# Base addresses of the operand tiles in a hybrid retention and attention layer

## The reference, cut to what matters

```python
h = rms_norm(x, g_pre_mix)
proj = h @ w_in                      # 1024 x 3072
rq, rk, rv, rg, aq, ak, av = split(proj)
ret = retention_branch(rq, rk, rv, rg, positions)          # 512 wide, chunks of 128
att = dilated_attention_branch(aq, ak, av, positions)      # 512 wide, dilations 1, 4, 16
mix = concatenate([ret, att]) @ w_out
x = x + rms_norm(mix, g_post_mix)
h = rms_norm(x, g_pre_ffn)
f = (silu(h @ w_gate) * (h @ w_up)) @ w_down               # D_FF = 2816
x = x + rms_norm(f, g_post_ffn)
```

## Time and profile before

| | |
|---|---|
| median of three runs | 2846.91 us |
| profiled execution, its own time | 2851.44 us |
| its span | 2849.7 us |
| TensorE busy | 2653.0 us, 93% |
| VectorE / ScalarE / GpSimd busy | 43% / 25% / 22% |
| mean granted TensorE clock | 0.963 |

### The profile page before, as it was taken

How to read it: one execution, slowest core, us unless ns; L and a number is a source line. 1 busy time by engine, 2 the same in 40 slices (tenths; PEclk the granted TensorE clock), 3 DMA queues, 4 the chain that set the end, 5 groups by cost and what they waited for, 6 DMA issues and landing times. The chain is left out here.

```text
span 2849.7 us, 36155 instructions
## 1 busy us (share of the span) xinstructions
PE 2653.0 (93%) x13096; PEld 2229.4 (78%) x13096; DVE 1231.6 (43%) x2271; ACT 722.1 (25%) x1402; POOL 627.2 (22%) x403
## 2 busy tenths in 40 slices
PE   6999999959989879997799999999999999999995
PEld 5888877749989757776588888888888888888884
DVE  5213455215655588885233333333354333333334
ACT  4112111116766522222211111111121111111111
POOL 1793544112344166663000000000010000000000
PEclk8999999979999989999899999999999999999998
DMA  4321233255335335553611111111352111111103
GB/s 164 97 73 61 79 110 110 96 140 128 103 102 172 115 112 178 175 179 123 243 45 45 59 59 44 44 44 45 117 185 82 45 44 54 64 44 44 44 15 103
DMA packets 220448, 269.66 MB, mean 95 GB/s; under 512 B 12224, under 2 KB 164672, under 8 KB 220096
## 3 DMA queue, kind: packets, MB, share of 16 engines
q1 hardware_dynamic: 220352, 268.42, 30.0%
HBM read 188.29 MB, written 80.08 MB: 94 GB/s over the span
## 5 line engine op out<-in xcount | busy, mean ns | idle before, releaser
L1418 PE MATMUL ff_psum_gu<-ff_h_hi,ff_w_hi 128*128 128x512 f32 x1408 | 550.5, 391 | 21.7 <-DMA ff_h_lo<-h_lo 21.7
L1418 PE MATMUL ff_psum_gu<-ff_h_lo,ff_w_hi 128*128 128x512 f32 x1408 | 550.1, 391 | 0.0
L1418 PE MATMUL ff_psum_gu<-ff_h_hi,ff_w_lo 128*128 128x512 f32 x1408 | 550.0, 391 | 0.0
L1523 POOL TENSOR_TENSOR ff_ssq<-ff_ssq,ff_minus_half 128x1 f32<-128x1 f32 x16 | 14.4, 905 | 1467.0 <-DVE ff_ssq L1564 1467.0
L1544 DVE TENSOR_TENSOR ff_gated<-ff_gated,ff_psum_gu 128x512 f32<-128x512 f32 x88 | 60.5, 687 | 628.8 <-PE ff_psum_gu L1418 628.8
L1418 PEld LDWEIGHTS ff_psum_gu<-ff_h_hi,ff_w_hi 128*128 128x128 f32 x1408 | 265.6, 189 | 77.6 <-issue 18.6
L327 PE MATMUL pr_psum_acc<-pr_hT_hi,pr_w_hi 128*128 128x512 f32 x768 | 304.6, 397 | 12.4 <-DVE pr_w_lo L234 12.4
L1418 PEld LDWEIGHTS ff_psum_gu<-ff_h_hi,ff_w_lo 128*128 128x128 f32 x1408 | 265.5, 189 | 55.3
L1418 PEld LDWEIGHTS ff_psum_gu<-ff_h_lo,ff_w_hi 128*128 128x128 f32 x1408 | 265.5, 189 | 55.0
L327 PE MATMUL pr_psum_acc<-pr_hT_lo,pr_w_hi 128*128 128x512 f32 x768 | 302.3, 394 | 0.0
L327 PE MATMUL pr_psum_acc<-pr_hT_hi,pr_w_lo 128*128 128x512 f32 x768 | 302.0, 393 | 0.0
(11 more groups left out here) (159 smaller groups left out, 3969.6 us busy)
## 6 DMA issues: line engine op xcount, KB each, us to landing
ff_raw<-in_w_gate SPq DMA_DIRECT2D x22, 1024.0 KB, 5.4
ff_raw<-in_w_up SPq DMA_DIRECT2D x22, 1024.0 KB, 7.8
ff_down_raw<-in_w_down SPq DMA_DIRECT2D x22, 1024.0 KB, 4.9
projT<-pr_rows SPq DMA_DIRECT2D x64, 256.0 KB, 2.4
att_out<-at_orow SPq DMA_DIRECT2D x192, 66.0 KB, 1.7
mx_att_in<-att_out SPq DMA_DIRECT2D x16, 792.0 KB, 4.8
pr_w_raw<-in_w_in SPq DMA_DIRECT2D x24, 512.0 KB, 4.3
nt_xin<-in_x SPq DMA_DIRECT2D x16, 512.0 KB, 5.0
```

The source lines that it names most:

```text
L1418: last = nc.tensor.matmul(gu_ps[:, tile, n], w[:, n, k, cols], h[:, k, t], start=i == 0, stop=i == 3 * KT - 1)
L1523: nc.gpsimd.tensor_tensor(ssq[:, c], ssq[:, c], minus_half[:], ALU.pow).then_inc(rooted, 1)
```

## The change

Four gap tiles are allocated (one in projection, three in the FFN), which nothing reads or writes, and two tiles of `mix` are declared further up. No instruction is added, removed or put elsewhere.

```diff
@@ project
         raw = m.sb("w_raw", [P, KT, P])
+        m.sb("gap", [P, 64])
         w_hi = m.sb("w_hi", [P, 2, KT, P], F32R)
         w_lo = m.sb("w_lo", [P, 2, KT, P], F32R)
@@ mix
         w_lo = m.sb("w_lo", [P, KT, DM], F32R)
+        mT_hi = m.sb("mT_hi", [P, 2, KT, P], F32R)
+        mT_lo = m.sb("mT_lo", [P, 2, KT, P], F32R)
         ident = m.sb("ident", [P, P])
...
         mixT = m.sb("mixT", [P, 4, P])
-        mT_hi = m.sb("mT_hi", [P, 2, KT, P], F32R)
-        mT_lo = m.sb("mT_lo", [P, 2, KT, P], F32R)
@@ ffn
         raw = m.sb("raw", [P, 2, KT, PW])
+        m.sb("gap0", [P, 96])
         w_hi = m.sb("w_hi", [P, 2, KT, PW], F32R)
         w_lo = m.sb("w_lo", [P, 2, KT, PW], F32R)
+        m.sb("gap1", [P, 32])
         down_raw = m.sb("down_raw", [P, TILES, DM])
         down_hi = m.sb("down_hi", [P, TILES, DM], F32R)
         down_lo = m.sb("down_lo", [P, TILES, DM], F32R)
         gated = m.sb("gated", [P, TILES, GROUP])
+        m.sb("gap2", [P, 112])
         a_hi = m.sb("a_hi", [P, UG, TILES, GROUP], F32R)
         a_lo = m.sb("a_lo", [P, UG, TILES, GROUP], F32R)
```

## The result

The changed kernel takes 2877.28 us (median of 4 runs, 2875.53 to 2883.28) against 2847.88 us before; the ratio is 1.0102, 95% interval 1.0079 to 1.0125. The profiled execution's span is 2881.5 us against 2849.7. The forecast was no change (2846.5); the time lies inside the range of 8 in 10, on the slower side.

What follows compares the result with a forecast made beforehand. TensorE was taken to bound projection and FFN, VectorE to pace mix. Terms of 0 for projection and FFN, -0.4 us for mix and 0 for moved operands took the median 2846.91 to 2846.5 us; range 2815 to 2893 us.

Steps and rivals of the forecast that it cites:

- The step to price by: Projection and FFN: price a matmul by its time from start to start, 226.7 ns, not by its duration of about 391.
- I take 0 for all three: Projection, gate and up, and down: the gaps' new differences change no step; 0 us, within bounds of -113 to +63.
- a coarse difference only shifts when the two reads are close: Projection and FFN: reason for the 0; differences of 64 bytes or more don't change how often weight load and moving read meet.
- a start off a multiple of 64: Mix's output product: its 234.1 ns step put down to a difference below 64 bytes or mT's start off 64.
- slower rival: Projection and FFN: unequal differences down to 64 bytes raise steps towards 234.1 ns; +63 us in full, 2910 us; chance 0.28.
- The one unequal row in the trace: Mix's output product before the change: operands 352 bytes apart by 512, step 234.1 ns against 226.7 elsewhere.
- if the unit is 256 bytes: Case of the slower rival: projection keeps its step, both FFN products pay; +46 us, 2893 us.
- faster rival: Projection and FFN: equal remainders collide, so the 13.3 ns extra falls to 2.3; -93 us, 2754 us; chance 0.20.
- one faster stage: Case of the faster rival: one stage alone gains, -25 us (projection, 2822), -46 (gate and up) or -23 (down).
- Mix: Mix's output product: step falls from 234.1 to 226.7 ns, mostly hidden in a wait; -0.4 us, bounds 0 and -5.2.
- Moved operands of other engines cost 0: VectorE and ScalarE split and copy the same tiles at other starts; 0 us.

Runs made afterwards that it cites:

- e4: Kernel before with all of projection's tiles 32 bytes further and all of the FFN's 96, both operands still at a difference of 0; ratio 0.9999.
- e3: Gaps resized against the kernel before, for differences by 256 bytes of 192 (projection), 96 (gate and up), 128 (down), 192 (mix); 2899.35 us, ratio 1.0185.
- e11: The changed kernel with gaps of 64 elements everywhere, so every stationary-to-moving difference is 256 bytes; ratio 1.0002 against the kernel before.
- the map: Table of steps by stationary-to-moving difference by 256 bytes, from runs with other gap sizes or sliced tiles against the kernel before; 226.7 to 234.2 ns.
- e10: Kernel before with each down matmul of 512 columns split into two of 256, addresses as before; 2875.27 us, ratio 1.0099.
- e8: Only the low weights (w_lo) of projection and of gate and up moved 128 bytes further, against the kernel before; ratio 1.0093.
- e14: Gate and up's 24 matmuls grouped in eights by operand pair, with its w_lo 128 bytes further, against the kernel before; ratio 1.0030.
- e15: Only gate and up's low moving tile (h_lo) moved 128 bytes further, in the old order, against the kernel before; ratio 1.0024.
- e7: Stationary tiles sliced from wider ones, for differences of 8 bytes (projection), 16 (FFN) and 4 (mix), against the kernel before; 2875.54 us, ratio 1.0099.
- e9: Both low tiles (weights and moving) of projection and of gate and up moved 128 bytes further, against the kernel before; ratio 1.0091.

## Why the prediction was wrong

- *The step to price by* held: 226.7 from the windows was the right number, the stages that TensorE sets were the right ones, and the loss is the change of that step times the count (32.8 us worked out, 32.3 in the FFN).
- *The step that failed* is "I take 0 for all three", with its reason that a coarse difference only shifts when the two reads are close, and its reading that what remains is a start off a multiple of 64. e4 shows that such a start costs nothing; e3, e11 and the map show that the unit is 256 bytes and that, of the 13 unequal differences tried, all but 240 (0.4 to 1.6 ns) and, for half of the FFN, 16 cost 2 to 7.5 ns. Gate and up (384, that is 128 by 256) rose by 6.6 ns and down (448, that is 192) by 2.3. Of mix's 256 + 64 + 32 it was the 96 that counted. For projection the 0 came true, but not by the reason given: 256 is a whole unit and so no difference at all, which the prediction had only as a case of its slower rival. The one unequal row in the trace said as much without the argument: it was the nearest row, and the value taken was not that row's.
- *The slower rival* had the mechanism and, in "if the unit is 256 bytes", the right outcome for projection. Its price was too high: it gave every unequal difference 7.4 ns and so 46 us for the two FFN products. Down's 192 is a cheap one (2.3 ns), and gate and up pays 6.6; together 32.8.
- *The faster rival* is refuted over the 14 differences of the map: none steps below 226.7. Its premise, that the 13.3 ns at equal remainders are a meeting of two reads, isn't shown: they come once per matmul with its load (e10), and no address tried gives them back. Its sum also shows a slip in the range, which was to take in one faster stage: gate and up alone would be 2801 us, below the 2815.
- *Mix* was right in its result: the step fell to 226.7 (227.7 with the uneven start of each product) and nothing came of it. The wait that took the gain was another than the one named: `hT_lo`, with 0.3 us a chunk, and not `w_out`. VectorE sets the pace, as was said.
- *Moved operands of other engines cost 0*: right (e11).
- *The rule of the Trainium skill* (TensorE: Matmul & The Clock Gate, "Step-by-step: what each phase is for"; SBUF — State Buffer, "Who interferes with whom") that a weight load takes no read bandwidth from the running matmul and that TensorE waits on no one: by it no address would matter, and the trace disagrees, by 2 to 7 ns a matmul that addresses alone make.

What is shown is that the step depends on where the moving tile starts against its own weights and against the next ones (e8, e14, e15). That two reads of the same memory meet is the natural reading, and no run sees them. What decides between two rhythms at one set of addresses (e7, e3 and the changed kernel) and e9's single steps stays open.

## What to carry to other kernels

Where a stage is a dense stream of float32r matmuls, read the step from start to start, not the duration, and compare it between stages with the same shape: a step that differs has a cause, here where two tiles lie. Give the stationary and the moving tile, and all tiles that take turns in either role, starts that are equal by 256 bytes (a difference of 256 or 512 is as good as 0); a small tile put ahead of one of them can cost 1 to 2% of such a kernel. And where the trace holds one row of the new kind, price the change by it.

## What the runs showed of the hardware that was not expected

- A float32r matmul of 512 columns at 2.4 GHz steps at 226.7 ns with equal remainders by 256 bytes, and at 229 to 234 with most others. Moving the moving tile alone does it too (e15, 234.0 in the step that reads it). At 1.2 GHz the step was 427 at mix's difference as well.
- The steps go in fixed cycles: two or seven steps long at 128, three at 192 and 160, seven at 96, and all steps equal (233.3) at 64. At 128 the two cycles differ in their mean (233.3 and 232.4), and one kernel can pass from one to the other (e3, the changed kernel).
- At a difference of 16 bytes the same code ran at 226.7 ns for 750 us and, after one break of 1.58 us, at 233.3 for the rest.
- A matmul with its own weight load takes 13.3 ns more than its columns at the best addresses, whether 256 or 512 of them stream (e10).
